# Hybrid decoder trunk on one core: another order at the beginning, the gate chain cut in two, and the gate products as two 64-row halves

## The reference, cut to what matters

```python
u = (rmsnorm(x) @ w_in)                      # xa, ga, q, f, i, g: six times 512 columns
xc = conv_b + sum(xpad[:, j:j + T] * cw[j] for j in range(4))
xh = xc.reshape(Bn, T, 8, 64)                # 8 blocks of 64 channels
r  = sigmoid(einsum('bthi,hij->bthj', xh, w_ra) + b_ra)
ig = sigmoid(einsum('bthi,hij->bthj', xh, w_rx) + b_rx)
log_a = -8.0 * r * softplus(-lam)
bt = sqrt(-expm1(2.0 * log_a)) * ig * xc
hs = scan(h = exp(log_a) * h + bt)           # along the tokens
y_a = hs * gelu(ga)
```

## Time and profile before

| | before |
|---|---|
| median of 3 runs | 2497.25 us |
| the profiled execution | 2496.15 us, its span 2494.5 us |
| mean granted clock of PE | 0.986 of 2.4 GHz |
| PE busy | 2396.7 us (96%), 15842 matmuls |
| DVE busy | 940.7 us (38%), 1593 instructions |
| ACT busy | 632.5 us (25%), of it 48 table loads of 1.28 us |
| POOL busy | 284.3 us (11%) |
| chain that ended last | PE 91%, DVE 5%, ACT 2% |

### The profile page before, as it was taken

How to read it: one execution, slowest core, us unless ns; L and a number is a source line. 1 busy time by engine, 2 the same in 40 slices (tenths; PEclk the granted TensorE clock), 3 DMA queues, 4 the chain that set the end, 5 groups by cost and what they waited for, 6 DMA issues and landing times.

```text
span 2494.5 us, 38619 instructions
## 1 busy us (share of the span) xinstructions
PE 2396.7 (96%) x15842; PEld 2147.5 (86%) x15842; DVE 940.7 (38%) x1593; ACT 632.5 (25%) x1189; POOL 284.3 (11%) x276
## 2 busy tenths in 40 slices
PE   5999999999999999999899999999999999999995
PEld 4777777788888888888798899899999999999995
DVE  6665664421121121223765666534211211211224
ACT  4344344321131120222334234422201201201210
POOL 0000001212212212222000000000100000010010
PEclk9999999999999999999999999999999999999998
DMA  5323234344444444454432222232232222222223
GB/s 178 120 99 105 102 103 169 128 150 150 128 151 151 127 151 151 129 203 151 121 101 76 69 69 86 81 136 85 86 100 84 84 98 87 84 90 95 84 84 109
DMA packets 88145, 284.10 MB, mean 114 GB/s; under 512 B 15856, under 2 KB 19056, under 8 KB 88048
## 3 DMA queue, kind: packets, MB, share of 16 engines
q1 hardware_dynamic: 41472, 151.01, 18.6%
q0 software_dynamic: 27648, 100.68, 12.5%
q10 hardware_dynamic: 18928, 31.03, 3.5%
HBM read 171.07 MB, written 111.62 MB: 113 GB/s over the span
## 4 chain that ended last, share of the span: by engine, by line
PE 91%; DVE 5%; ACT 2%; ACTq 1%; issue 1%; DVEq 0%
PE bank L438 29%; PE bank L440 28%; PE bank L439 28%; PE aux L572 1%; PE aux L500 1%; DVE a_lo L1272 1%; ACT s_in L637 1%; PE aux L528 1%; PE aux L551 1%; PE aux L550 1%; DVE xc L1230 1%; PE aux L505 1%; DVE xy L1005 0%; DVE xy L1159 0%; PE aux L451 0%
## 5 line engine op out<-in xcount | busy, mean ns | idle before, releaser
L438 PE MATMUL bank<-a_hi,w_hi 128*128 128x358 f32 (+3 forms) x2560 | 923.3, 361 | 38.3 <-DVE a_lo L1272 20.4
L439 PE MATMUL bank<-a_lo,w_hi 128*128 128x358 f32 (+3 forms) x2560 | 906.4, 354 | 0.0
L440 PE MATMUL bank<-a_hi,w_lo 128*128 128x358 f32 (+3 forms) x2560 | 906.2, 354 | 0.0
L438 PEld LDWEIGHTS bank<-a_hi,w_hi 128*128 128x128 f32 x2560 | 485.6, 190 | 88.8 <-POOL w_lo L393 22.5
L440 PEld LDWEIGHTS bank<-a_hi,w_lo 128*128 128x128 f32 x2560 | 486.3, 190 | 43.6
L439 PEld LDWEIGHTS bank<-a_lo,w_hi 128*128 128x128 f32 x2560 | 486.2, 190 | 43.4 <-issue 2.2
L438 PE MATMUL bank<-b_hi,w_hi 128*128 128x358 f32 (+3 forms) x1280 | 452.1, 353 | 0.0
L439 PE MATMUL bank<-b_lo,w_hi 128*128 128x358 f32 (+3 forms) x1280 | 450.6, 352 | 0.0
L440 PE MATMUL bank<-b_hi,w_lo 128*128 128x358 f32 (+3 forms) x1280 | 450.4, 352 | 0.0
L1360 DVE TENSOR_TENSOR xy<-xy,bank 128x356 f32 (+5 forms) x160 | 94.1, 588 | 559.3 <-PE bank L440 559.3
L637 ACT ACTIVATE a_hi<-tmp 128x356 f32 (+5 forms) x160 | 88.3, 552 | 830.5 <-DVE tmp L1349 830.5
(11 more groups left out here) (159 smaller groups left out, 1414.0 us busy)
## 6 DMA issues: line engine op xcount, KB each, us to landing
w_st<-in_wall SPq DMA_DIRECT2D x96, 512.0 KB, 4.3
kept_hi<-w_hi SPq DMA_DIRECT2D x96, 512.0 KB, 5.1
kept_lo<-w_lo SPq DMA_DIRECT2D x96, 512.0 KB, 5.9
w_hi<-kept_hi POOLq DMA_DIRECT2D x96, 512.0 KB, 3.9
w_lo<-kept_lo POOLq DMA_DIRECT2D x96, 512.0 KB, 4.6
xs<-in_xT ACTq DMA_DIRECT2D x8, 536.0 KB, 6.7
xy<-in_xT ACTq DMA_DIRECT2D x8, 536.0 KB, 7.9
xs<-in_xT ACTq DMA_DIRECT2D x16, 256.0 KB, 6.6
```

The lines of the kernel that those rows point to most:

```text
L438: pe.matmul(ps, wh, xh, start=(j == 0), stop=False)
L439: pe.matmul(ps, wh, xl, start=False, stop=False)
L440: mm = pe.matmul(ps, wl, xh, start=False, stop=(j == 7))
```

## The change

**The beginning.** SP and ACT share the loads: SP loads weight block 0, the odd blocks of x of tile 0, weight block 1, the odd blocks of tile 1, then `ident` and the gate weights. ACT issues 8 loads of x, then does `w_hi` of block 0, 8 `a_hi`, `w_hi` of block 1, 8 `a_hi`, and a Sqrt of one column into `sink` (which brings the Sqrt table) ahead of the squares. The small Exps move behind the Sqrts of `RS`. On DVE `rest_of_prep` and the two memsets of pass 0 move behind the convolution of head 0; the wait for the masks moves behind the reciprocals of `RS`.

**The chain.** The piece GATE ends after the Tanh. `GA` (slot 18, or 27 in pass 1) holds ACT's Sqrt and DVE's `u`, `a`, `v`, `igx`; `GB` (slot 0 or 1 of the next head) holds `bt`, the scan and the copies.

**The gate products.** One buffer `w_gate` replaces the two. For its rows 0 to 63 it holds `w_ra` in columns 0 to 63 and `w_rx` in columns 64 to 127; for rows 64 to 127 the other way round. A product takes 64 rows of `xc` and gives both gates of 64 channels, the one of `w_rx` on the opposite partitions. ACT reads each bank twice, 64 partitions each, with a bias that is turned likewise.

The diff, cut to its lines:

```diff
@@ schedule tables
+GATE_A_SLOT, GATE_B_SLOT = [18, 27], [0, 1]
@@ schedule
+                    if i < HEADS and s == GATE_A_SLOT[p]:
+                        pieces.append(("GA", i))
+                    if i >= 1 and s == GATE_B_SLOT[p]:
+                        pieces.append(("GB", i - 1))
@@ build: buffers
+sink = sb("sink", [P, 1])
...
-w_ra = sb("w_ra", [P, 4, P])
-w_rx = sb("w_rx", [P, 4, P])
+w_gate = sb("w_gate", [P, 4, P])
+b_rx_turned = sb("b_rx_turned", [P, 4])
@@ sync (SP queue)
-    for j in range(2):
-        load(j, j)
+    def load_x0(t, b):
+        c0, w = TILES[0][t]
+        sync.dma_start(xs[:, b, c0:c0 + w], xT[b, :, c0:c0 + w]).then_inc((x_in2 if t else x_in)[b], 16)
+    load(0, 0)
+    for b in range(1, KB, 2):
+        load_x0(0, b)
+    load(1, 1)
+    for b in range(1, KB, 2):
+        load_x0(1, b)
+    sync.dma_start(ident[:, :], ident_d).then_inc(const_in, 16)
+    for h in range(2):
+        r_, o_ = slice(64 * h, 64 * h + 64), slice(64 - 64 * h, 128 - 64 * h)
+        sync.dma_start(w_gate[r_, :, r_], wra_d[r_, :, r_]).then_inc(const_in, 16)
+        sync.dma_start(w_gate[r_, :, o_], wrx_d[r_, :, r_]).then_inc(const_in, 16)
+        sync.dma_start(b_rx_turned[o_, :], par_d[r_, PC["b_rx"]:PC["b_rx"] + 4]).then_inc(const_in, 16)
@@ tensor: piece
-            pe.wait_ge(const_in, 16 * 3)
...
+            if n == 0:
+                pe.wait_ge(const_in, 16 * 7)
@@ tensor: piece, GATE
+            if n == 0:
+                pe.wait_ge(const_in, 16 * 7)
...
-                for g, wt in enumerate((w_ra, w_rx)):
-                    ps = open_bank(a + 2 * t + g)
-                    pe.matmul(ps[:, 0:w], wt[:, i, :], xc[:, c0:c0 + w], start=True,
+                for h in range(2):
+                    r_ = slice(64 * h, 64 * h + 64)
+                    ps = open_bank(a + 2 * t + h)
+                    pe.matmul(ps[:, 0:w], w_gate[r_, i, :], xc[r_, c0:c0 + w], start=True,
@@ scalar: loads of x
-        for b in range(KB):
+        for b in range(0, KB, 2):
...
-    act.dma_start(ident[:, :], ident_d).then_inc(const_in, 16)
-    act.dma_start(w_ra[:, :, :], wra_d).then_inc(const_in, 16)
-    act.dma_start(w_rx[:, :, :], wrx_d).then_inc(const_in, 16)
@@ scalar: piece, GATE and GA
-                for g, (dst, b) in enumerate(((ta, "b_ra"), (ig, "b_rx"))):
-                    u = a + 2 * t + g
+                for h in range(2):
+                    u = a + 2 * t + h
+                    r_, o_ = slice(64 * h, 64 * h + 64), slice(64 - 64 * h, 128 - 64 * h)
+                    act.wait_ge(const_in, 16 * 7)
...
-                    fn(dst[:, c0:c0 + w], aux[u % 4][:, 0:w], ACT.Sigmoid,
-                       bias=col(b, i)).then_inc(aux_free[u % 4], 1)
-            for t in range(NT[p]):
-                drained(act, a + 2 * t)
+                    fn(ta[r_, c0:c0 + w], aux[u % 4][r_, 0:w], ACT.Sigmoid,
+                       bias=par[r_, PC["b_ra"] + i:PC["b_ra"] + i + 1])
+                    fn(ig[r_, c0:c0 + w], aux[u % 4][o_, 0:w], ACT.Sigmoid,
+                       bias=b_rx_turned[o_, i:i + 1]).then_inc(aux_free[u % 4], 1)
+            for u in range(a, a + 2 * NT[p]):
+                drained(act, u)
...
+        elif name == "GA":
@@ scalar: beginning
-    for n in range(2):
-        round_weights(n)
+    round_weights(0)
...
-    act.wait_ge(prep, 3)
-    fn(sp[:, 0, :], sp[:, 0, :], ACT.Exp, scale=-1.0).then_inc(prep_act, 1)
-    fn(lbv[:, 0, :], lbv[:, 0, :], ACT.Exp).then_inc(prep_act, 1)
@@ scalar: beginning
+            if p == 0 and t == 0:
+                round_weights(1)
...
+            act.wait_ge(consts, 5)
+            fn(sink[:, :], eps[:, :], ACT.Sqrt)
@@ scalar: walk over the schedule
+                if p == 0:
+                    act.wait_ge(prep, 3)
+                    fn(sp[:, 0, :], sp[:, 0, :], ACT.Exp, scale=-1.0).then_inc(prep_act, 1)
+                    fn(lbv[:, 0, :], lbv[:, 0, :], ACT.Exp).then_inc(prep_act, 1)
...
-                if name not in ("RS", "FN", "R", "OT", "Y"):
+                if name not in ("RS", "FN", "R", "OT", "Y", "GB"):
@@ vector: piece, GA and GB
-        elif name == "GATE":
+        elif name == "GA":
+            a = AUX[(p, "GATE", i)]
...
-            for t in range(NT[p]):
-                drained(dve, a + 2 * t + 1)
+            for u in range(a, a + 2 * NT[p]):
+                drained(dve, u)
...
+        elif name == "GB":
...
+            T, E, I = ta[:, 0:th], ea[:, 0:th], ig[:, 0:th]
@@ vector: beginning
-            rest_of_prep()
...
-        dve.memset(near[:, :, :], 0.0)
-        dve.memset(attn[:, :], 0.0).then_inc(zeroed, 1)
-        dve.wait_ge(zeroed, p + 1)
-        dve.wait_ge(smp_in, 16 * (8 + 11 * p))
+        if p:
+            dve.memset(near[:, :, :], 0.0)
+            dve.memset(attn[:, :], 0.0).then_inc(zeroed, 1)
+            dve.wait_ge(zeroed, p + 1)
@@ vector: walk
+                dve.wait_ge(smp_in, 16 * (8 + 11 * p))
@@ vector: walk
+                if un == (0, XA, nt - 1) and p == 0:
+                    rest_of_prep()
+                    dve.memset(near[:, :, :], 0.0)
+                    dve.memset(attn[:, :], 0.0).then_inc(zeroed, 1)
+                    dve.wait_ge(zeroed, 1)
...
-                if name not in ("RS", "NF"):
+                if name not in ("RS", "NF", "GATE"):
```

More of the change, by code:

```diff
@@ L157, in aux_uses @@
 def aux_uses(p, name):
-    if name in ("FN", "FY", "R", "N", "Y"):
+    if name in ("FN", "FY", "R", "N", "Y", "GA", "GB"):
         return 0
@@ L592, in _ @@
                     for name, i in pieces:
-                        if name not in ("FN", "FY", "R", "N", "Y"):
+                        if name not in ("FN", "FY", "R", "N", "Y", "GA", "GB"):
                             piece(p, name, i)
```

## The result

The changed kernel takes **2501.66 us** (median of 19 runs, 2497.18 to 2505.47) against 2497.01 for the kernel before on the same chips (19 runs, 2495.18 to 2499.20): ratio 1.0019, interval 1.0012 to 1.0026. It is slower by about 5 us where 5 less were forecast. The profiled execution took 2502.49 us, its span is 2500.8. PE's busy time is nearly the same; ACT has nine table loads more, 57 of them.

The account below looks back on a forecast made before the run. TensorE was taken as the bound almost everywhere, except where VectorE's and ScalarE's chain binds: the beginning and pass 0's gate chain. Terms 6.3 + 0.8 + 0.4 - 2.2 = 5.3 us less gave 2492.0 us, range 2487 to 2500.

Parts of the forecast that it names:

- Part 1: Kernel start: shared loads and earlier splits bring the restart behind 1/rms to 47.9, 6.3 us sooner.
- Part 2: Preparation moved between head 0's convolution and w_lo of block 4: TensorE waits 2.2 us, once.
- Part 3: Split gate chain in pass 0: the q wait goes, L1 starts 0.2 us sooner per head, 0.8 us in all.
- the pace is 0.58: ScalarE's gate reads in pass 0: eight 64-row reads start 0.58 us apart and end at +5.9.
- the far bound: Gate reads of pass 0 without overlap, 0.69 us each: a loss of 0.6 us per head.
- rival B: Half reads overlap less, at 0.69 us: pass 0's chain ends 0.8 later, pass 1 waits 0.3 more; 2496.4 us, chance 0.15.
- So the wait is not removed: it moves to L1: Pass 0 heads: TensorE's 2.0 us q wait becomes a wait for q*f at L1, which starts at +23.8.
- Rival A: Clock falls at pass 0's L1 waits: about 2494 to 2503.6 us; chance 0.18 one or two heads, 0.08 three or four.
- Part 4: Half-width gate products overlap: 1.1 us a head only lengthens pass 0's L1 wait; pass 1 gains 0.4 in all.
- Rival C: TensorE keeps all the halves save, no wait at L1 or in the six units: 2475.5 us, chance 0.05.

Follow-up runs that it names:

- e6: The kernel before with the new beginning alone, the preparation in its new place included: 2489.30 us, ratio 0.9969 to the kernel before.
- e7: The changed kernel with full-width gate products and reads, and the preparation back behind the sums of squares: 2475.56 us, ratio 0.9918 to the kernel before.
- e8: The changed kernel with full-width gate products, each bank still read as two halves of 64 partitions, none crossing: 2490.74 us, ratio 0.9982 to the kernel before.
- e5: The changed kernel with pass 0's second chain part (bt, scan, copies) at slot 6, behind q*f: 2489.86 us, ratio 0.9976 to the kernel before.
- e4: The changed kernel with three unread extra products filling most of pass 0's L1 wait: 2496.87 us, ratio 1.0000 to the kernel before.
- e2: The kernel before with the half-width gate products and reads alone, chain undivided, old beginning: 2524.53 us, ratio 1.0109 to the kernel before.
- e12: The kernel before with one unused one-column buffer declared, no instruction changed: 2493.78 us, ratio 0.9987 to the kernel before.

## Why the prediction was wrong

The measured 2501.66 lies above the range (2487 to 2500) and on the other side of no change.

- **Part 1, the beginning: right.** Forecast a restart at 47.9 and 6.3 us; measured 46.83 and 7.4. The first product came at 11.37 (11.0), and the two a_lo that run beside a split of POOL took 2.3 and 2.9 us where the other 14 took 0.74 each. e6 bears the gain out.
- **Part 2, the preparation: right.** Forecast a wait of 2.2, measured 2.00; e7 has it removed.
- **Part 3, "the pace is 0.58": this step failed.** I took the pace of two full-width reads of another function for reads of 64 partitions and took the case without overlap for the far bound, while the rows of 32 partitions shown above had no overlap. The bound was true: 0.70 in the changed kernel and in e8. It put u at +10.5 in place of +9.45 and L1 at +24.9 in place of +23.8. The sum had 0.2 gained a head; it lost 0.85, as rival B said (0.6).
- **"So the wait is not removed: it moves to L1": the mechanism was right**, the wait is there with its releaser, and e5 shows that DVE's chain makes it. It was 3.6 where 3.2 was forecast. By the prediction's own steps it was 2.9: L1 at +23.8, and PE there at 24.04 - 2.03 - 1.1 = +20.9.
- **The clock: the second failed step, and the one that made the kernel slower and not the same (e4: ratio 1.0000).** Rival A had mechanism and price (1.5 to 2.9 a head), but at four heads a chance of 0.08, because the earlier trace rows seemed to show a boundary between 2.76 and 3.44. In the very profile that I had, the clock fell behind the fourth q wait of 2.0 (335 to 340); I had read the clock behind the first alone. Kept warm, the same kernel is 4.8 us faster (e4). Nor did I see that A and B belong together: if the reads are slower, the wait is longer, and the clock is surer to fall. The forecast, B's 4.4 and A's lower price of 4 x 1.5 together are 2492.0 + 4.4 + 6.0 = 2502.4, against the measured 2501.66. That they come so near is in part luck. With what was measured in place of each term the sum is 7.4 (beginning) - 2.0 (preparation) - 3.4 (later L1) - 2.4 (pass 1, next point) - 4.8 (clock, by e4) = -5.2, so 5.2 us slower, against the measured 4.65.
- **Part 4, the halves.** 1.1 us forecast for PE in pass 0, 1.4 measured (the second product of the next unit starts at +2.2 in place of +3.7), and that it would only lengthen the wait was right. For pass 1 I had 0.1 a head gained; the same distance is +4.3 in place of +3.8, 0.6 lost, because a read of 358 columns took 0.57 and not 0.45. Rival C was near about PE in pass 0 (eight records in 1.99 us in place of 3.6) and wrong about the time. The Trainium skill, TensorEngine Tiling (Array Packing), says under Performance Considerations that tiling does not speed up the evacuation of PSUM; the trace agrees, ACT's reads go from +1.2 to +6.8 in place of +1.1 to +4.3. That pass 1 has cover for the longer reads was right for the changed kernel, but e2 shows that it is the split that gives it.
- **Not in the prediction at all:** the place of `b_hi`. It does not explain the difference between the two kernels, which both lie beside the line, but 3 us were to be had there.
- The chance of slower by over 0.2% was 0.07. The ratio, 1.0019, falls just short of that line, so "within 0.2%" is what came.

Open: why reads of a part of the partitions do not follow each other more closely; whether full-width sigmoid reads of PSUM would do so at 0.58 (in these kernels the products, 0.86 apart in pass 0 and 0.60 in pass 1, always hold them up); and why keeping PE warm gives 7.5 us between two profiles but 4.8 between the medians.

## What to carry to other kernels

Before an engine is made faster, ask who waits for whom behind it: where another engine ends last, what is saved becomes a longer wait, and a longer wait of TensorE may cost its clock for the products behind it. Take the releasing chain apart first (here the split) and leave the fast engine's work alone. Read a clock behind every wait of a kind and in two executions, not behind one. When kernels differ in a place that the edit doesn't touch, compare their buffers' addresses.

## What the runs showed of the hardware

- Reads of PSUM by ACT (Sigmoid with a bias) of 64 partitions and 512 columns start 0.70 us apart, of 358 columns 0.57, crossing or not (changed kernel and e8); each takes as long as one of 128 partitions (0.69). Half the partitions cost the full price, and they lose the overlap of about 0.1 us that most back-to-back instructions of 128 partitions have (598 of 620 pairs in the kernel before).
- Float32 products on the two 64-row halves of the array overlap: eight records in 1.99 us where full-width ones take 3.6.
- The granted clock fell to 1.2 GHz with every wait of 3.6 us (8 of 8, two executions), with 7 of 16 waits of 2.0 (four executions), with one of four of 2.5 to 3.0 (e8), and with none that was filled to 1.0 (e4).
- The MLP's products of 512 and 496 columns run 0.5% faster (442 per 100 us in place of 440) when `b_hi` and `b_lo` lie 32 bytes further on, by the declarations on a multiple of 64 bytes and not 32 past one (e12).
